# Differential attention in a trunk step on one core: three units' jobs in one half slot, the sample stream's steps in one half slot too

## The reference: what is computed

```python
s = jnp.einsum('bqhcd,bkhcd->bhcqk', q, k).astype(jnp.float32) * (DIFF_DH ** -0.5)
visible = (k_pos // CHUNK)[None, :] <= (q_pos // CHUNK)[:, None]
s = jnp.where(visible, s, -1e30)
p = jax.nn.softmax(s, axis=-1)
a = p[:, :, 0] - lam * p[:, :, 1]
return jnp.einsum('bhqk,bkhv->bqhv', a.astype(v.dtype), v)
```

## Time and profile before

| | |
|---|---|
| median of 3 runs | 1635.96 us (1634.15 to 1637.27) |
| profiled execution | 1634.28 us |
| its span, first to last instruction | 1632.5 us |
| mean granted TensorE clock | 0.969 |
| TensorE matmul busy | 1506.7 us (92%) |
| VectorE, ScalarE, GpSimd busy | 819.9, 650.5, 356.7 us |
| stage of the change | about 778 to 1195 us of the span |

### The profile page before, as it was taken

One profiled execution on the slowest core, in us unless ns is written; L12 is line 12 of the kernel. 1 busy time (PEld: TensorE's weight loads), 2 busy tenths in 40 slices (PEclk: granted clock), 3 DMA queues, 4 the chain that ended last, 5 costly groups with the idle time before them and its releaser, 6 DMA issues.

```text
span 1632.5 us, 21317 instructions
## 1 busy us (share of the span) xinstructions
PE 1506.7 (92%) x7820; PEld 1127.9 (69%) x7820; DVE 819.9 (50%) x1391; ACT 650.5 (40%) x1069; POOL 356.7 (22%) x197
## 2 busy tenths in 40 slices
PE   4999999999999999999989899999999699999981
PEld 2675677567757775778777677777778578877771
DVE  3242251225122512221775857644255699988884
ACT  5222221221222122312435354543233378888871
POOL 1342123212411331133332112111332100000002
PEclk8999999999999999999999999999999599999995
DMA  9433453445344534432431254145650699999975
GB/s 347 132 92 128 153 169 92 140 141 169 91 142 141 168 91 142 143 92 78 159 129 40 75 159 154 29 155 183 201 152 39 221 317 390 394 385 388 387 301 206
DMA packets 158091, 290.31 MB, mean 178 GB/s; under 512 B 15083, under 2 KB 40859, under 8 KB 157733
## 3 DMA queue, kind: packets, MB, share of 16 engines
q1 hardware_dynamic: 154246, 278.47, 50.2%
q0 software_dynamic: 3744, 10.49, 1.8%
HBM read 251.55 MB, written 40.52 MB: 179 GB/s over the span
## 4 chain that ended last, share of the span: by engine, by line
PE 30%; DVE 9%; DMA 8%; issue 2%; ACT 2%; SPq 1%; POOL 0%; DVEq 0%; ACTq 0%; POOLq 0%
PE pj L93 7%; PE pj L95 7%; PE pj L94 7%; DMA m_raw<-w 5%; DVE d_tmp L2188 2%; PE d_B L2460 1%; PE d_B L2479 1%; PE d_B L2487 1%; DMA ring_raw<-w_out 1%; PE d_B L2521 1%; DMA d_kc<-cache_diff_k 1%; ACT m_hi L1390 1%; PE d_B L2469 1%; PE d_B L1565 1%; DMA ring_raw<-w_br_diff 1%
## 5 line engine op out<-in xcount | busy, mean ns | idle before, releaser
L93 PE MATMUL pj<-ring_hi,hT_hi 128*128 128x512 f32 x880 | 370.4, 421 | 14.7 <-POOL ring_lo L479 7.2
L95 PE MATMUL pj<-ring_hi,hT_lo 128*128 128x512 f32 x880 | 347.2, 395 | 0.0
L94 PE MATMUL pj<-ring_lo,hT_hi 128*128 128x512 f32 x880 | 346.0, 393 | 0.0
L479 POOL TENSOR_TENSOR ring_lo<-ring_raw,ring_hi 128x1024 fp32r<-128x1024 f32 x79 | 190.2, 2408 | 557.8 <-ACT ring_hi L545 557.8
L545 ACT ACTIVATE ring_hi<-ring_raw 128x1024 fp32r<-128x1024 f32 x79 | 83.4, 1058 | 425.6 <-DMA ring_raw<-w_in 360.2
L1469 DVE TENSOR_TENSOR m_lo<-m_raw,m_hi 128x1024 fp32r<-128x1024 f32 x188 | 223.6, 1222 | 25.6 <-ACT m_hi L1390 23.6
L93 PEld LDWEIGHTS pj<-ring_hi,hT_hi 128*128 128x128 f32 x880 | 167.4, 190 | 69.2 <-issue 36.5
L1390 ACT ACTIVATE m_hi<-m_raw 128x1024 fp32r<-128x1024 f32 x188 | 194.4, 1058 | 27.1 <-DMA m_raw<-w 24.7
L95 PEld LDWEIGHTS pj<-ring_hi,hT_lo 128*128 128x128 f32 x880 | 166.6, 189 | 37.4
L94 PEld LDWEIGHTS pj<-ring_lo,hT_hi 128*128 128x128 f32 x880 | 167.6, 190 | 28.7 <-issue 1.0
L1919 POOL TENSOR_TENSOR ring_lo<-ring_raw,ring_hi 128x1024 fp32r<-128x1024 f32 x37 | 91.4, 2472 | 316.9 <-ACT ring_hi L1939 316.9
(11 more groups left out here) (341 smaller groups left out, 2387.0 us busy)
## 6 DMA issues: line engine op xcount, KB each, us to landing
m_raw<-w SPq DMA_DIRECT2D x188, 512.0 KB, 10.6
ring_raw<-w_in SPq DMA_DIRECT2D x72, 512.0 KB, 3.8
r_S<-state_ret SPq DMA_DIRECT2D x64, 256.0 KB, 4.7
r_ada_raw<-w_ada SPq DMA_DIRECT2D x16, 1024.0 KB, 6.9
o_state_s<-r_S SPq DMA_DIRECT2D x64, 256.0 KB, 4.7
a_raw<-w_ada SPq DMA_DIRECT2D x8, 1024.0 KB, 12.2
ring_raw<-w_in SPq DMA_DIRECT2D x32, 256.0 KB, 3.2
ring_raw<-w_br_ret SPq DMA_DIRECT2D x16, 512.0 KB, 4.2
```

The source lines that it names most:

```text
L93: pe.matmul(out, s_hi, m_hi, start=start, stop=False)
L94: pe.matmul(out, s_hi, m_lo, start=False, stop=False)
L95: return pe.matmul(out, s_lo, m_hi, start=False, stop=stop)
L479: pool.tensor_tensor(lo[:, p], raw[:, p], hi[:, p].bitcast(F32), ALU.subtract).then_inc(lo_done, 1)
```

## The change

- Units: in the first half S of unit u is due at 76 + 4u instead of 84 + 4u. A is due two periods after S, P three: 8 and 12 half slots in the first half, 6 and 9 in the second. So P of unit u - 3, S of unit u and A of unit u - 2 are due at the same half slot, in this order on TensorE (P was behind S). VectorE takes P before the maxima; ScalarE squares it two half slots later instead of three.
- Stream: C is due 4 after K, B 8, V 16, so that V, B, C and K of different samples lie in one half slot, in this order. The second stream starts at 244 instead of 246. ScalarE's exponents of C come in C's own half slot ahead of the copies of K, VectorE's scaling one half slot later.
- The rows of the first half are turned 2 to 4 half slots later, the last output at 298 instead of 302.
- The rotations of group K1 are 4 half slots later (m from 11 instead of 7).

```diff
-        self.first, self.period = ((84, 4), (194, 3))[i]
-        self.cache = (152, 246)[i]
-        self.turns = ((34, 38, 42, 46, 50), (158, 162, 170, 178, 186))[i], ((64, 68, 72, 76, 80), (188, 190, 192, 196, 198))[i]
-        self.out = ((248, 252, 256, 264, 272), (280, 282, 284, 286, 302))[i]
+        self.first, self.period = ((76, 4), (194, 3))[i]
+        self.cache = (152, 244)[i]
+        self.turns = ((38, 42, 46, 50, 54), (158, 162, 170, 178, 186))[i], ((68, 72, 74, 78, 82), (188, 190, 192, 196, 198))[i]
+        self.out = ((248, 252, 256, 264, 272), (280, 282, 284, 286, 298))[i]
...
     def turned(self, h):
-        return self.unit(h, 6)
+        return self.unit(h, 2 * self.period)
 
     def valued(self, h):
-        return self.unit(h, 8)
+        return self.unit(h, 3 * self.period)
...
     def s_scored(self, h):
-        return self.stream(h, 3)
+        return self.stream(h, 4)
 
     def s_turned(self, h):
-        return self.stream(h, 9)
+        return self.stream(h, 8)
 
     def s_valued(self, h):
-        return self.stream(h, 17, 8, DEC_B // 2)
+        return self.stream(h, 16, 8, DEC_B // 2)
...
-                    if some(half.valued(s - 3)):
-                        n = half.valued(s - 3)
+                    if some(half.valued(s - 2)):
+                        n = half.valued(s - 2)
...
+                    if some(half.s_scored(s)):
+                        s_exp(i, half.s_scored(s))
                     if some(half.keys_turned(s)):
                         take_keys(i, half.keys_turned(s))
                     if some(half.out_turned(s)):
                         take_O(i, half.out_turned(s))
-                    if some(half.s_scored(s - 2)):
-                        s_exp(i, half.s_scored(s - 2))
...
+                    if some(half.valued(s)):
+                        take_o(i, half.valued(s))
                     if some(half.scored(s)):
                         for a in (1, 0):
                             maximum(i, half.scored(s), a)
-                    if some(half.valued(s)):
-                        take_o(i, half.valued(s))
...
-                    if some(half.s_scored(s - 3)):
-                        s_scale(i, half.s_scored(s - 3))
+                    if some(half.s_scored(s - 1)):
+                        s_scale(i, half.s_scored(s - 1))
...
-                    elif 7 <= m <= 15 and m % 2:
-                        rotate(*norm, (m - 7) // 2)
+                    first = 11 if name == "K1" else 7
+                    if first <= m <= first + 8 and m % 2:
+                        rotate(*norm, (m - first) // 2)
...
+                    if some(half.valued(s)):
+                        values(i, half.valued(s))
                     if some(half.scored(s)):
                         scores(i, half.scored(s))
-                    if some(half.valued(s)):
-                        values(i, half.valued(s))
...
+                    if some(half.s_scored(s)):
+                        s_scores(i, half.s_scored(s))
                     if some(half.keys_turned(s)):
                         turn_keys(i, half.keys_turned(s))
-                    if some(half.s_scored(s)):
-                        s_scores(i, half.s_scored(s))
```

More of the change, by code:

```diff
@@ L1178, in __init__ @@
                 i = at.i
+                if some(at.valued(h)):
+                    add(2, "P", i, at.valued(h))
                 if some(at.scored(h)):
@@ L1181, in __init__ @@
                         add(m, "S", i, at.scored(h), m)
-                if some(at.valued(h)):
-                    add(2, "P", i, at.valued(h))
                 if some(at.s_valued(h)):
@@ L1195, in __init__ @@
                     add(0, "B", i, at.s_turned(h))
+                if some(at.s_scored(h)):
+                    add(2, "C", i, at.s_scored(h))
                 if some(at.keys_turned(h)):
@@ L1198, in __init__ @@
                     add(1, "K", i, at.keys_turned(h), 1)
-                if some(at.s_scored(h)):
-                    add(2, "C", i, at.s_scored(h))
 RING, LEAD, EARLY, PIECES = 12, 4, 12, 12 * N_EXP
```

## The result

The kernel after takes 1641.5 us (median of 20 runs, 1636.0 to 1643.8), the kernel before beside it 1634.7: the ratio is 1.0033, its 95% interval 1.0024 to 1.0042. By the ratio the change costs 5.4 us (3.9 to 6.9). The forecast was 1632.8 in a range from 1626 to 1641: too low, and on the wrong side.

What follows compares the result with a forecast made beforehand. TensorE was taken as the bound, busy 343 of 366 us. Terms -4.3 + 2.6 - 6.4 + 3.2 + 1.4 + 4.5 - 4.2 = -3.2 gave 1632.8 us on the median's scale, range 1626 to 1641.

Steps and rivals of the forecast that it cites:

- Rival A: Waits for VectorE's answers inside the half slot take over: +7.8, 1640.6 us; chance 0.25.
- The signs named beforehand: Right: no take_o wait over 2 us at 132 to 150, none at 304, stands at 80 and 280, fewer slow half slots.
- A's sign: L2469 or L2487 waiting for VectorE in many half slots would show the forecast wrong.
- Part 1: Fewer TensorE interruptions: 69 merges give 2.8 us, earlier small-matmul starts 1.5; sum -4.3, bounds 0 and -8.8.
- Parts 2 and 3: First units eight half slots earlier, +2.0 and 0.6 slow clock; K1's rotations behind half 0's last scores, -6.4.
- The stand at 80: TensorE stands at half slot 80, so 84 begins near 851.3 instead of 847.7: +2.0, and 0.6 for slow clock.
- Part 4: Units of the second half: bank round at 242 and 245 +1.5, small misses 0.8, holds 1.0; +3.2, bounds +1 and +6.
- Part 5, first stream: VectorE's fold late behind a rotation: +2.0 at 188, GpSimd hold +0.7, small waits of 1.3 go; +1.4.
- The term for half slot 188: First stream: the fold is late behind a rotation where a K row follows in bank 0, +2.0.
- Part 5, second stream: Outputs share the stream's half slots: four misses +2.8, 0.35 at 248, 280 +0.9, slow clock +1.3; +4.5, bounds 0 and +8.
- The four outputs that were to miss by 0.7 each: Second stream: turned outputs sharing the half slot, with the fold behind them, miss by 0.7 each: +2.8.
- Part 6: Last output at 298 and last sample values at 284 close the wait at half slot 304: -4.2, bounds -1 and -4.7.

Runs made afterwards that it cites:

- experiment 5: Kernel after with K1's rotations back at m = 7 (half slots 134 to 150): 1644.3 us, ratio 1.0064 to the kernel before.
- experiment 11: Kernel of experiment 1 with K1's rotations back in their old place (m from 7): 1636.4 us, ratio 1.0008 to the kernel before.
- Experiment 3: Kernel after with the K row of half slot 188 in bank 2 instead of 0: 1638.6 us, ratio 1.0015 to the kernel before.
- experiment 8: Kernel after with the last output back at half slot 302: 1641.0 us, ratio 1.0031 to the kernel before.
- experiment 10: Kernel of experiment 1 with the last output back at half slot 302: 1634.3 us, ratio 0.9989 to the kernel before.
- experiment 1: Kernel after with the sample stream as before, second stream from 246, all else new: 1630.7 us, ratio 0.9965 to the kernel before.
- experiment 6: Kernel after with the first unit due at half slot 80 instead of 76: 1643.1 us, ratio 1.0053 to the kernel before.
- experiment 2: Kernel after with units, rows and K1's rotations as before; stream new, last output at 298: 1644.8 us, ratio 1.0056 to the kernel before.
- experiment 4: Kernel after with the first output of half 1 at half slot 278 instead of 280: 1636.9 us, ratio 1.001 to the kernel before.

## Why the prediction was wrong

**The place of the error.** Its parts gave gains of 14.9 and losses of 11.7; a few microseconds more on the losses turn the sign. Rival A named mechanism and place. That its time, 1640.6, is 0.9 from the measured one is luck: it counted 13 answers of VectorE missed by 0.6 beside ring pieces, and what came is three long stands, four of 0.44 and the half clock behind the long ones. What spoke against it was that scores hide the round trip in half slots 200 to 239. They do there. The stream's half slots aren't like them. The signs named beforehand couldn't tell the two apart: no wait over 2 for take_o between 132 and 150 (the longest is 1.97), none at 304, stands at 80 and 280 all came, and A's sign, waits for VectorE in many half slots, came too.

**Part 1 (-4.3): too large by some 1.6.** Where the merged job had another interruption directly behind it, a merge is worth the 0.02 that the earlier trace rows showed, not 0.04 and more. The starts of L93 at half slots 230 and 233 of before and of after (before has the values at 232 by themselves):

```profile
1044.80 0.47 PE L93 MATMUL pj<-ring_hi,hT_hi 128*128 128x512 f32 x1
...
1049.26 0.47 PE L93 MATMUL pj<-ring_hi,hT_hi 128*128 128x512 f32 x1
```

```profile
1049.24 0.47 PE L93 MATMUL pj<-ring_hi,hT_hi 128*128 128x512 f32 x1
...
1053.68 0.47 PE L93 MATMUL pj<-ring_hi,hT_hi 128*128 128x512 f32 x1
```

4.46 and 4.44: 0.02 for values joined to scores and turned tiles, and nothing of the 0.09 by which scores were said to start late. Read in the same way, the merged turns of half 0 gave some 0.08 and the stream's 0.03 each. With 16, 16 and 37 of them, that is 2.7 instead of 4.3. The starts also say why. Only in half 0 did the merged job have a slower half slot of its own behind it (half slot 103 takes 0.78 in before, 0.68 in after). In half 1 and in the stream it mostly lay directly ahead of another interruption, so there was no exit to save: between 40 and 310 the half slots of more than 0.85 us fell from 141 to 86, those of 0.74 to 0.82 only from 75 to 73, where some 70 fewer were forecast.

**Parts 2 and 3 (+2.6 and -6.4): mechanism right, both mis-sized.** The stand at 80 came, and half slot 84's scores within 0.4 us of the forecast, but not the clock behind: 0.6 was counted, and 6.8 us at half clock, up to 3.4, came. K1's rotations gain 4.2 by experiment 5's trace (2.8 to 5 by its times), 3.5 to 7 by experiment 11, where 6.4 were forecast: new waits of 2.0 at half slot 136 ('s kind: take_o behind an operation of 2.28 that a ring piece holds) and short ones in four more half slots take back more than the 2.5 that was counted. From 40 to 150 the forecast was -4.4 with its 16 merges. The traces have +0.7, of which 0.9 is P(15), done at 148 now and at 152 before; so -0.2 like for like. These two parts failed by 4.2 us, up to 2.8 of it the clock; in the other traces with these units, where the clock was low for 3.4 to 10.2 us here, the stretch takes 124.3 to 126.6, so some 2 us of the 4.2 hang on it.

**Part 4 (+3.2; its items add up to 3.3): right in its largest term.** At 242 and 245 the gaps are 2.20 where before spends 1.04 and 0.62 in two interruptions: 0.68 more for each after the exit saved, forecast 0.75 less 0.04. The GpSimd holds counted at 1.0 and the small misses at 0.8 didn't come: the waits of A for d_o in 1002 to 1066 us are 0.5 in all; two waits of together 1.5 for ScalarE's exponents went, and one at 198 grew from 0.8 to 1.8. This last one is the stream's doing, and the forecast had no term for it: half slots 194 to 240 take 63.9 in before, 62.5 in all four kernels with the new units and the old stream, and 63.7 in after. So the merged units gain 1.4 here, and the stream takes 1.2 of it back.

**Part 5, first stream (+1.4): the step that failed most.** The term for half slot 188 was right (2.0 forecast, 2.44 measured), the one for a GpSimd hold, 0.7, wasn't: the hold fell on the rotation ahead of the fold of 176 and made 2.54. And no slow clock was counted behind either, though the earlier trace rows shows one behind a long stand: two of 3.4 us cost up to 3.4. 2.4 + 2.5 + 3.4 is 8.3; less P(15) that left the stretch (0.9), the small waits that went (1.3) and the merges (0.5) it is 5.6, measured 5.0. The forecast by the same count is -0.1. Experiment 3 takes 2.9 of it out by one digit.

**Part 5, second stream (+4.5): right within 1 us.** 2.9 from 250 to 288 and 0.9 of the 2.3 from 240 to 250. Within it, 280 stood 3.4 for 3.7. The four outputs that were to miss by 0.7 each miss by 0.44 (the wait ahead of K at 252, 256, 264 and 272 is 1.8 in all).

**Part 6 (-4.2): right in size, the credit misplaced.** -4.5 was measured. The prediction listed both causes, the output at 298 and the last sample values at 284. Experiments 8 and 10 show that the second does most: the reload is issued 0.2 ahead of half slot 284's first matmul instead of 0.2 behind that of 287, and ScalarE's split of the ring piece starts 2.5 ahead of half slot 303 instead of 0.1. Moved alone, the output gives 0.7 to 2.3 by the traces. So a part of the loss in the stream comes back here. That the stands ahead of it help too, because TensorE comes later to the same load, is not shown apart from the earlier reload.

**Together** the forecast's terms from half slot 240 on were right within 1 us each. The error is in two places, 40 to 150 and 150 to 194, of about 4 and 5 us, and up to 6 of these 9 are, in this execution, the half clock behind stands. So the step that failed is the price of the first stream and of the stand at 80: the rotation ahead of the fold of 176 and the half clock behind the stands at 176 and 188 stood in the sum at 0.7 and at nothing.

## What to carry to other kernels

Before jobs of one chain are put into one interruption of TensorE, list for each half slot what stands ahead of the answering copy in VectorE's and ScalarE's queues. The copy itself takes 0.3 to 0.6 us, a rotation ahead of it 2.7 and more, a table load with five copies 3.8, and the merge that it is paid with saves 0.02 to 0.08. And price each long stand at up to 1.7 more than its length: in the 13 traces, between half slots 1 and 304, the clock was halved for at least 3.4 us in or right behind 36 of 39 stands of 2.35 us and more, and at 15 of 47 between 1.5 and 2.2. Here the version that keeps the old stream and takes the rest of the change (experiment 1) is the fastest measured, 0.9965 of before by six runs; three neighbours of it, each one edit away and with 12 runs each, lie at 0.9989 to 1.0008.

## What the runs showed of the hardware that was not expected

The clock's answer to a stand isn't a fixed line. Behind after's stands of 2.4 us and more (176, 188, 280) and those of 304 in before and experiments 1 and 10 it was halved for 3.4 us, at 304 of experiment 10 for 6.8; behind after's stand of 2.1 with 0.7 soon after it, at half slot 80, for 6.8 too. Stands of 2.67 at half slot 176 of experiments 5 and 6, and of 3.03 at 304 of experiment 11, had no low clock behind them. TensorE's wait of 1.9 at half slot 240 is in all kernels; before, after and seven others keep the full clock behind it, experiments 1, 2, 4 and 10 don't (in experiment 1 the clock is 0.72 over these 6 us):

```profile
1056.00:1062.00 6.00, 4.72 (x20) 4.10 (x21) 1.39 (x4) 3.08 (x10) 0.00 (x0) 0.72 0.83 260
```

That run took 1635.5 where the median of experiment 1 is 1630.7. This stretch costs 1.7 of the 5, and from half slot 310 on it took 482.1 where before took 479.0. So a single execution of these kernels can stand 5 us off its median, as much as the whole change is worth, and a trace has to be compared stretch by stretch and not by its span.
